# Expert weights of a mixture-of-experts layer in 168 transfers of 2 MB, one for each pair of units, in place of 336 transfers of 1 MB

## The chip, the cores and the metric

The kernel runs on one core of a Trainium2 chip. The time is the device time of one execution in microseconds (us), as the median of several runs. The five engines are TensorE (PE, with its weight load PEld), VectorE (DVE), ScalarE (ACT), GpSimd (POOL) and SyncE (SP). SP computes nothing here: it issues transfers from device memory (HBM) to the on-chip memory (SBUF), and its queue is written SPq.

## The reference

The kernel computes two layers of a decoder trunk on 256 tokens of width 1024, in float32. Each layer has a mixer (a gated delta rule on 4 heads and a stick-breaking attention on 8 heads) and then a channel mixer. In layer 0 that is a dense SwiGLU of width 2816. In layer 1 it is a SwiGLU of 8 experts of width 3584, each token going to the best 2:

```
def moe_swiglu(h, router_w, w_gate, w_up, w_down):
    logits = (xt @ router_w).astype(jnp.float32)
    top_val, top_idx = lax.top_k(logits, TOP_K)
    gates = jax.nn.softmax(top_val, axis=-1)
    combine = jnp.einsum("nk,nke->ne", gates, jax.nn.one_hot(top_idx, N_EXPERTS, dtype=jnp.float32))
    y = jnp.zeros((B * T, D), dtype=jnp.float32)
    for e in range(N_EXPERTS):
        y = y + combine[:, e:e + 1] * swiglu(xt, w_gate[e], w_up[e], w_down[e]).astype(jnp.float32)
```

The three weights of the experts are 8 x 3 x 1024 x 3584 numbers of 4 bytes, 352 MB in all, and each is read once.

## The kernel before

Everything is written out by hand: each engine has its own program, and semaphores join them. The expert stage starts after the output projection of layer 1. It works on one expert after another, and cuts its 3584 hidden columns into four chunks of 8, 8, 8 and 4 tiles of 128 (`MOE_TILES`). TensorE gathers up to 88 tokens of an expert, multiplies them by the gate and up weights of a chunk (`m_in`, L1119), later by its down weights (`m_down`, L1143), and at times transposes the result (L1157), adds it back to the tokens (`scatter_piece`, L1175, eight pieces in the first part of each expert but the first one's) and gathers the next expert's tokens (L1049).

The weights come in units of 1 MB: 128 partitions by 2048 numbers, 32 calls of TensorE each. `unit_queue` fixes the order of the 336 units, which is the order of their transfers and of their use. Sixteen buffers (`N_UNIT`) hold them in turn: twelve lie in the tensor `ring`, which the mixers and the dense layer used before in four slots of three units, and four in the tensor `late`, which the mixer of layer 1 leaves free later. The first 16 units are issued as these places come free (`first_free`), and unit n after that when TensorE has finished unit n - 16 (`unit_used`).

There is a second condition for unit n. The program of TensorE is longer than the engine holds, and its instructions are themselves brought in while it runs, in blocks; the kernel counts blocks of `PAGE` = 256 instructions. `page_turns` marks one call of TensorE shortly behind the start of each block, and this call raises the semaphore `page_turn`. `UNIT_TURN` says for each unit behind which such turn the transfer into its buffer may be issued, and lets at most two units go behind one turn:

```
if has_signal and signal_every == UNIT_CALLS:
    earliest = unit_turn[-TURN_UNITS] + 1 if len(unit_turn) >= TURN_UNITS else 1
    unit_turn.append(max(len(turns) + 1, earliest))
```

Worked out, this gives 172 turns. Behind each of them two units may go, but behind the turns 1, 14, 36, 50, 58, 79, 101, 114, 123 and 144 one. So behind turns 2 to 13 an odd unit and the next even one go together, behind turns 15 to 35 an even unit and the next odd one, and so on in turn.

Of the kernel before, what the change touches and what calls it, by code (L numbers as in the profile page):

```python
# [30 lines left out]
P = 128  # L31
D = 1024
# [16 lines left out]
SLOT = 2 * KD * FC + (FC // P) * D  # L49
NSLOT = 4  # L50
# [4 lines left out]
MOE_TILES = (8, 8, 8, 4)  # L55
# [16 lines left out]
FIRST_MOE = 2 * N_MIX + FFN_CH  # L72

UNIT = 2048
N_OWN = NSLOT * SLOT // UNIT
N_UNIT = N_OWN + 4
# [21 lines left out]
ROUND_UNITS = len(UNITS)  # L98
# [57 lines left out]
PAGE_TURNS, UNIT_TURN = page_turns()  # L156
# [52 lines left out]
def build(nc, x_in, consts, norm_mix_pre, norm_mix_post, norm_ffn_pre, norm_ffn_post, w_in, conv_w,  # L209
          dn_a_log, dn_dt_bias, dn_norm_w, sb_norm_w, w_out, ffn_gate, ffn_up, ffn_down, router_w,  # L210
          moe_gate, moe_up, moe_down, out):
    with ExitStack() as ctx:
        def sb(name, cols, dt=F32):
            return ctx.enter_context(nc.sbuf_tensor(name, [P, cols], dt))

        def sem(name):
            return ctx.enter_context(nc.semaphore(name))
# [7 lines left out]
        ring = sb("ring", NSLOT * SLOT)  # L225
# [7 lines left out]
        late = sb("late", (N_UNIT - N_OWN) * UNIT + 512)  # L233
# [73 lines left out]
        at = [0]  # L307
# [44 lines left out]

        ring_landed = [sem(f"ring_landed{i}") for i in range(NSLOT)]
        ring_used = sem("ring_used")
        unit_landed = [sem(f"unit_landed{i}") for i in range(N_UNIT)]
        unit_used = sem("unit_used")
        x_landed = [sem(f"x_landed{t}") for t in range(TT)]
        consts_landed, rows_landed, heads_landed, router_landed = (
# [45 lines left out]
        page_turn = sem("page_turn")  # L404
# [24 lines left out]
        def gate_up_down(n):  # L429
# [3 lines left out]
            d = s[:, 2 * KD * FC:SLOT].rearrange("p (i d) -> p i d", i=FC // P)  # L433
            return g, u, d

        def unit_of(n):

            i = n % N_UNIT
            if i < 3:
                return ring[:, 3 * SLOT + i * UNIT:3 * SLOT + (i + 1) * UNIT]  # L440
            if i < 6:
                return ring[:, (i - 3) * UNIT:(i - 2) * UNIT]
            if i < 10:
                return late[:, (i - 6) * UNIT:(i - 5) * UNIT]
            return ring[:, SLOT + (i - 10) * UNIT:SLOT + (i - 9) * UNIT]

        def gate_ks(c, j):

            nk = 2 * 8 // MOE_TILES[c]
            return range(j * nk, (j + 1) * nk)  # L450

        def gate_unit(n, c):
            return unit_of(n).rearrange("p (k f) -> p k f", f=MOE_TILES[c] * P)

        def down_unit(n):
            return unit_of(n).rearrange("p (i d) -> p i d", d=D)
# [9 lines left out]
        def per_round(r, n, a_round):  # L466
            return r * a_round + n
# [47 lines left out]
        def _(sp_):  # L515
# [44 lines left out]
            for c in range(FFN_CH):  # L560
                free_slot(FIRST_FFN + c)
                f = slice(c * FC, (c + 1) * FC)
# [2 lines left out]

            def first_free(n):

                if n < 6:
                    sp_.wait_ge(ring_used, FIRST_MOE - NSLOT + 1 + n // 3)
                elif n == 6:  # L570
                    sp_.wait_ge(dno_ps, DEPTH)
                    sp_.wait_ge(sb_ss, DEPTH * TT)
                elif n >= 10:
                    sp_.wait_ge(ring_used, FIRST_MOE - 1 + (n - 10) // 3)

            def moe_loads(r, first):
                for (kind, e, c, j), n in UNITS.items():
                    if first and n < N_UNIT:
                        first_free(n)
                    elif first:  # L580
                        sp_.wait_ge(unit_used, n - N_UNIT + 1)
                        sp_.wait_ge(page_turn, UNIT_TURN[n - N_UNIT])
                    else:
                        sp_.wait_ge(unit_used, per_round(r, n - N_UNIT + 1, ROUND_UNITS))
                    if kind == "d":
                        lo = (MOE_AT[c] + 2 * j) * P
                        dst = down_unit(n)
                        src = moe_down[0, e][lo:lo + 2 * P, :].rearrange("(i p) d -> p i d", p=P)
                    else:
                        f = slice(MOE_AT[c] * P, (MOE_AT[c] + MOE_TILES[c]) * P)  # L590
                        ks = gate_ks(c, j)
                        dst = gate_unit(n, c)
                        src = (moe_gate if kind == "g" else moe_up)[0, e][ks.start * P:ks.stop * P, f]\
                            .rearrange("(k p) f -> p k f", p=P)
                    sp_.dma_start(dst, src).then_inc(unit_landed[n % N_UNIT], 16)

            moe_loads(0, True)
            sp_.wait_ge(rounds_ready, 1)
            rounds = sp_.value_load(rounds_i[0:1, 0:1], min_val=1, max_val=3)
            with sp_.If(rounds > 1):  # L600
                with sp_.Fori(1, rounds) as r:
                    moe_loads(r, False)
# [9 lines left out]
        def _(pe):  # L612
# [479 lines left out]
                ins.then_inc(ohT_ps, 1)  # L1092

            def landed(r, n):
                pe.wait_ge(unit_landed[n % N_UNIT], per_round(r, 16 * (n // N_UNIT + 1), 16 * ROUND_UNITS // N_UNIT))

            def units_of(c, part):

# [1025 lines left out]
```

## Time and profile before

| | |
|---|---|
| median of 3 runs | 1599.26 us (1595.29 to 1600.52) |
| the profiled execution | 1602.32 us, its span 1600.5 us |
| granted TensorE clock, mean | 0.993 of full speed |
| PE busy | 1538.1 us, 96% of the span |
| expert stage, first to last call of L1119 and L1143 | about 642 us to 1582 us |

The span is the time from the first to the last instruction in the profile; the execution is 1.8 us longer than it. A busy PE is not PE at its peak, since matmuls overlap in it. An idle time "<-issue" is one in which the engine waited for nothing that the profile shows. The DMA share is the mean busy share of the 16 DMA engines; it can pass 1 by a little, since packets overlap.

### The profile page before, as it was taken

To read this page: it belongs to the slowest core of one execution; us is meant where nothing else is said; L and a number is where in the kernel's file an instruction comes from. 1 tells how busy PE (TensorE), PEld (TensorE's weight loads), DVE (VectorE), ACT (ScalarE), POOL (GpSimd) and SP (SyncE) were. 2 spreads that over 40 slices of the span, in tenths; PEclk is the share of its full clock that TensorE was granted. 3 is DMA by queue.
4 is the path that set the end of the run, shared out by engine and by line. 5 is a ranking of instruction groups with operands and counts; after the bars stand their busy time and mean duration, and the time that the engine had idled before them with its cause. 6 is when DMAs were issued, how large, how long until landed. Compare 5 with 4: busy or idle time off the path is not lost.

```text
span 1600.5 us, 54283 instructions
## 1 busy us (share of the span) xinstructions
PE 1538.1 (96%) x25845; PEld 1329.8 (83%) x25845; DVE 258.0 (16%) x489; ACT 179.0 (11%) x383; POOL 143.4 (9%) x167
## 2 busy tenths in 40 slices
PE   8999999999999999999999999999999999999998
PEld 7787587777687865989899999999999998998996
DVE  3433310000143435000010010010000000000002
ACT  3223120000231332100000000000000000000001
POOL 2243200000022532200000000000000000000000
PEclk9999999999999999999999999999999999999998
DMA  9213344444332145999999999999999999999970
GB/s 337 86 52 132 105 158 158 158 158 145 112 138 106 56 158 221 355 387 365 379 389 374 358 369 373 384 363 391 379 370 386 366 361 377 393 354 381 388 283 28
DMA packets 147947, 433.46 MB, mean 271 GB/s; under 512 B 9082, under 2 KB 33916, under 8 KB 147724
## 3 DMA queue, kind: packets, MB, share of 16 engines
q1 hardware_dynamic: 146720, 427.70, 71.6%
q8 instruction: 203, 3.33, 0.8%
q0 software_dynamic: 672, 2.14, 0.5%
q10 hardware_dynamic: 332, 0.13, 0.0%
q14 instruction: 20, 0.16, 0.0%
HBM read 428.89 MB, written 1.05 MB: 269 GB/s over the span
## 4 chain that ended last, share of the span: by engine, by line
PE 92%; issue 3%; DVE 2%; ACT 1%; POOL 1%; DMA 0%; ACTq 0%; DVEq 0%
PE ps L1119 35%; PE ps L1143 18%; PE ps L969 9%; PE ps L675 8%; PE ps L980 4%; PE ps L838 4%; PE ps L686 3%; PE ps L1175 2%; PE ps L1049 1%; PE ps L795 1%; PE ps L671 1%; PE ps L805 1%; PE ps L701 1%; PE ps L708 1%; PE ps L815 1%
## 5 line engine op out<-in xcount | busy, mean ns | idle before, releaser
L1143 PE MATMUL ps<-LT_sb,ring 128*64 128x88 f32 x5376 | 217.5, 240 | 11.4 <-issue 9.8
L1143 PEld LDWEIGHTS ps<-LT_sb,ring 128*64 128x64 f32 x5376 | 208.4, 137 | 21.1 <-issue 19.7
L1119 PE MATMUL ps<-wpost,ring 128*64 128x88 f32 x5376 | 215.4, 240 | 10.8 <-issue 9.2
L1119 PEld LDWEIGHTS ps<-wpost,ring 128*64 128x64 f32 x5376 | 207.8, 137 | 18.7 <-issue 16.8
L1119 PE MATMUL ps<-AT_sb,ring 128*64 128x88 f32 x5376 | 215.4, 240 | 7.7 <-issue 7.4
L1119 PEld LDWEIGHTS ps<-AT_sb,ring 128*64 128x64 f32 x5376 | 207.9, 137 | 16.2 <-issue 15.8
L969 PEld LDWEIGHTS ps<-hT_sb,ring 128*128 128x128 f32 x768 | 136.0, 190 | 24.7 <-issue 9.1
L969 PE MATMUL ps<-hT_sb,ring 128*128 128x256 f32 (+1 forms) x768 | 155.7, 362 | 0.0
L675 PE MATMUL ps<-hT_sb,ring 128*128 128x256 f32 x592 | 131.7, 380 | 0.0
L675 PEld LDWEIGHTS ps<-hT_sb,ring 128*128 128x128 f32 x592 | 111.1, 190 | 15.4 <-DVE late L1620 0.5
L1964 POOL TENSOR_SCALAR small<-small 128x1 f32<-128x1 f32 x16 | 3.9, 241 | 1204.9 <-ACT late L1498 935.5
L1479 ACT ACTIVATE BM<-ps 128x704 f32<-128x704 f32 (+1 forms) x32 | 21.9, 684 | 675.6 <-PE ps L1119 675.6
L1907 DVE TENSOR_TENSOR LT_sb<-BM,ps 128x704 f32<-128x704 f32 (+1 forms) x32 | 25.4, 793 | 417.0 <-PE ps L1119 417.0
L1119 PE MATMUL ps<-AT_sb,late 128*64 128x88 f32 x1792 | 72.1, 240 | 2.6 <-issue 2.6
L1143 PE MATMUL ps<-LT_sb,late 128*64 128x88 f32 x1792 | 72.5, 240 | 1.6 <-issue 1.2
L1119 PEld LDWEIGHTS ps<-AT_sb,late 128*64 128x64 f32 x1792 | 69.5, 137 | 5.4 <-issue 5.3
L1119 PE MATMUL ps<-wpost,late 128*64 128x88 f32 x1792 | 71.8, 240 | 2.0 <-issue 1.9
L1143 PEld LDWEIGHTS ps<-LT_sb,late 128*64 128x64 f32 x1792 | 69.6, 137 | 4.5 <-issue 4.3
L1119 PEld LDWEIGHTS ps<-wpost,late 128*64 128x64 f32 x1792 | 69.4, 137 | 4.3 <-issue 4.0
L1895 DVE SCALAR_TENSOR_TENSOR h_sb<-ps,small,h_sb 128x512 f32<-128x512 f32 x32 | 24.0, 751 | 294.8 <-PE ps L1175 290.3
L980 PE MATMUL ps<-ring,LT_sb 128*128 128x512 f32 x144 | 64.7, 592 | 0.0
L838 PE MATMUL ps<-ring,hT_sb 128*128 128x512 f32 x128 | 58.4, 607 | 1.7 <-ACT hT_sb L1432 1.7
(284 smaller groups left out, 1164.3 us busy)
## 6 DMA issues: line engine op xcount, KB each, us to landing
ring<-in_moe_w_gate SPq DMA_DIRECT2D x84, 1024.0 KB, 8.0
ring<-in_moe_w_up SPq DMA_DIRECT2D x84, 1024.0 KB, 8.0
ring<-in_moe_w_down SPq DMA_DIRECT2D x84, 1024.0 KB, 8.1
late<-in_moe_w_up SPq DMA_DIRECT2D x28, 1024.0 KB, 8.0
late<-in_moe_w_gate SPq DMA_DIRECT2D x28, 1024.0 KB, 8.9
late<-in_moe_w_down SPq DMA_DIRECT2D x28, 1024.0 KB, 7.8
ring<-in_ffn_w_gate SPq DMA_DIRECT2D x11, 1024.0 KB, 5.4
ring<-in_ffn_w_up SPq DMA_DIRECT2D x11, 1024.0 KB, 8.0
```

The source lines that it names most:

```text
L671: ins = mm(o[:, t * P:(t + 1) * P], w[:, k, col:col + P], hT[:, k, t * P:(t + 1) * P], start=(k == 0), stop=(k == KD - 1))
L675: ins = mm(o[:, 0:T], w[:, k, col:col + P], hT[:, k, :], start=(k == 0), stop=(k == KD - 1))
L686: ins = mm(o, hT[:, k, i * P:(i + 1) * P], w[:, k, col:col + 512], start=(k == 0), stop=(k == KD - 1))
L838: ins = mm(bank(4 + 2 * t + hf), mixT[:, k, t * P:(t + 1) * P], w[:, k, :], start=(k == 4), stop=(k == 3))
L969: ins = mm(bank(mt % 4)[:, which * T + lo:which * T + hi], w[:, k, i * P:(i + 1) * P], hT[:, k, lo:hi], start=(k == 0), stop=(k == KD - 1))
L980: ins = mm(bank(4 + 2 * t + half), ffn_hid[:, mt % 4, t * P:(t + 1) * P], d[:, i, half * 512:(half + 1) * 512], start=(mt == 0), stop=(mt ...
L1119: ins = mm(o[lo:lo + P // 2, :], w[:, i, m * P + lo:m * P + lo + P // 2], xgT[e % 2][:, k, :], start=(k == 0 and m % 4 == 0), stop=(k == K ...
L1143: ins = mm(o[lo:lo + P // 2, :], d[:, i, m * P + lo:m * P + lo + P // 2], moe_hid[:, 2 * j + i, :], start=(first and m % 4 == 0), stop=las ...
L1175: ins = mm(bank(6 + hf)[:, quarter * 256:(quarter + 1) * 256], onehotT[e % 2][:, t * P:(t + 1) * P], y_tok[:, (2 * hf + quarter) * 256:(2 ...
L1479: A(by_bank(moe_sg, c), tiles_of(0, c), ACT.Silu).then_inc(msg_ready, 1)
L1895: V.scalar_tensor_tensor(moe_yv[:, t, half(hf)], bank((6 if e < N_EXP - 1 else 2 * t) + hf), gate[:, t * N_EXP + e:t * N_EXP + e + 1], moe ...
L1907: V.tensor_tensor(by_bank(moe_hid, c), by_bank(moe_sg, c), tiles_of(2, c), ALU.mult).then_inc(mhid_ready, 1)
```

## The change

Two neighbouring units, n even and n + 1, become a pair. `pair_of` places the two side by side, and the order of the buffers moves for this: the first pair lies at the end of `ring`, the second at its start, the third and fourth in `late`, the others in the rest of `ring`. One transfer of 2 MB fills a pair, with the semaphore `pair_landed`; its rows in HBM are those of the two transfers before. It waits for the condition that the second unit of the pair had. TensorE waits once for a pair. The calls of TensorE and what they read of the weights stay the same, and so does the number of instructions in its program, 13638 as written, since the wait of the second unit rode on a matmul.

```diff
@@ -352,7 +352,7 @@
 
         ring_landed = [sem(f"ring_landed{i}") for i in range(NSLOT)]
         ring_used = sem("ring_used")
-        unit_landed = [sem(f"unit_landed{i}") for i in range(N_UNIT)]
+        pair_landed = [sem(f"pair_landed{i}") for i in range(N_UNIT // 2)]
         unit_used = sem("unit_used")
         x_landed = [sem(f"x_landed{t}") for t in range(TT)]
         consts_landed, rows_landed, heads_landed, router_landed = (
@@ -433,16 +433,16 @@
             d = s[:, 2 * KD * FC:SLOT].rearrange("p (i d) -> p i d", i=FC // P)
             return g, u, d
 
+        def pair_of(n):
+
+            i = n // 2 % (N_UNIT // 2)
+            if i in (2, 3):
+                return late[:, (i - 2) * 2 * UNIT:(i - 1) * 2 * UNIT]
+            at = (N_OWN - 2, 0)[i] if i < 2 else 2 * (i - 3)
+            return ring[:, at * UNIT:(at + 2) * UNIT]
+
         def unit_of(n):
-
-            i = n % N_UNIT
-            if i < 3:
-                return ring[:, 3 * SLOT + i * UNIT:3 * SLOT + (i + 1) * UNIT]
-            if i < 6:
-                return ring[:, (i - 3) * UNIT:(i - 2) * UNIT]
-            if i < 10:
-                return late[:, (i - 6) * UNIT:(i - 5) * UNIT]
-            return ring[:, SLOT + (i - 10) * UNIT:SLOT + (i - 9) * UNIT]
+            return pair_of(n)[:, n % 2 * UNIT:(n % 2 + 1) * UNIT]
 
         def gate_ks(c, j):
 
@@ -565,34 +565,35 @@
 
             def first_free(n):
 
-                if n < 6:
-                    sp_.wait_ge(ring_used, FIRST_MOE - NSLOT + 1 + n // 3)
-                elif n == 6:
+                if n < 4:
+                    sp_.wait_ge(ring_used, FIRST_MOE - NSLOT + 1 + n // 2)
+                elif n == 4:
                     sp_.wait_ge(dno_ps, DEPTH)
                     sp_.wait_ge(sb_ss, DEPTH * TT)
-                elif n >= 10:
-                    sp_.wait_ge(ring_used, FIRST_MOE - 1 + (n - 10) // 3)
+                elif n >= 8:
+                    sp_.wait_ge(ring_used, FIRST_MOE - 1 + (n - 8) // 4)
 
             def moe_loads(r, first):
                 for (kind, e, c, j), n in UNITS.items():
+                    if n % 2:
+                        continue
                     if first and n < N_UNIT:
                         first_free(n)
                     elif first:
-                        sp_.wait_ge(unit_used, n - N_UNIT + 1)
-                        sp_.wait_ge(page_turn, UNIT_TURN[n - N_UNIT])
+                        sp_.wait_ge(unit_used, n + 1 - N_UNIT + 1)
+                        sp_.wait_ge(page_turn, UNIT_TURN[n + 1 - N_UNIT])
                     else:
-                        sp_.wait_ge(unit_used, per_round(r, n - N_UNIT + 1, ROUND_UNITS))
+                        sp_.wait_ge(unit_used, per_round(r, n + 1 - N_UNIT + 1, ROUND_UNITS))
                     if kind == "d":
                         lo = (MOE_AT[c] + 2 * j) * P
-                        dst = down_unit(n)
-                        src = moe_down[0, e][lo:lo + 2 * P, :].rearrange("(i p) d -> p i d", p=P)
+                        dst = pair_of(n).rearrange("p (i d) -> p i d", d=D)
+                        src = moe_down[0, e][lo:lo + 4 * P, :].rearrange("(i p) d -> p i d", p=P)
                     else:
                         f = slice(MOE_AT[c] * P, (MOE_AT[c] + MOE_TILES[c]) * P)
-                        ks = gate_ks(c, j)
-                        dst = gate_unit(n, c)
-                        src = (moe_gate if kind == "g" else moe_up)[0, e][ks.start * P:ks.stop * P, f]\
-                            .rearrange("(k p) f -> p k f", p=P)
-                    sp_.dma_start(dst, src).then_inc(unit_landed[n % N_UNIT], 16)
+                        lo, hi = gate_ks(c, j).start * P, gate_ks(c, j + 1).stop * P
+                        dst = pair_of(n).rearrange("p (k f) -> p k f", f=MOE_TILES[c] * P)
+                        src = (moe_gate if kind == "g" else moe_up)[0, e][lo:hi, f].rearrange("(k p) f -> p k f", p=P)
+                    sp_.dma_start(dst, src).then_inc(pair_landed[n // 2 % (N_UNIT // 2)], 16)
 
             moe_loads(0, True)
             sp_.wait_ge(rounds_ready, 1)
@@ -1092,7 +1093,9 @@
                 ins.then_inc(ohT_ps, 1)
 
             def landed(r, n):
-                pe.wait_ge(unit_landed[n % N_UNIT], per_round(r, 16 * (n // N_UNIT + 1), 16 * ROUND_UNITS // N_UNIT))
+                if n % 2 == 0:
+                    pe.wait_ge(pair_landed[n // 2 % (N_UNIT // 2)],
+                               per_round(r, 16 * (n // N_UNIT + 1), 16 * ROUND_UNITS // N_UNIT))
 
             def units_of(c, part):
 
```

How the order of SP's transfers moves at the start of the expert stage, where the first 16 units go into free places (rows of SP, equal ones that follow each other merged; the shape is partitions x rows x numbers). Before:

```order
L595 DMA ring<-in_moe_w_gate 128x2x1024 [waits ring_used] x4
L595 DMA ring<-in_moe_w_up 128x2x1024 [waits ring_used] x2
L595 DMA late<-in_moe_w_up 128x2x1024 [waits sb_ss,dno_ps]
L595 DMA late<-in_moe_w_up 128x2x1024
L595 DMA late<-in_moe_w_gate 128x2x1024 x2
L595 DMA ring<-in_moe_w_gate 128x2x1024 [waits ring_used] x2
L595 DMA ring<-in_moe_w_down 128x2x1024 [waits ring_used] x4
L595 DMA ring<-in_moe_w_up 128x2x1024 [waits page_turn,unit_used] x4
```

And after the change:

```order
L596 DMA ring<-in_moe_w_gate 128x4x1024 [waits ring_used] x2
L596 DMA late<-in_moe_w_up 128x4x1024 [waits sb_ss,dno_ps]
L596 DMA late<-in_moe_w_up 128x4x1024
L596 DMA ring<-in_moe_w_gate 128x4x1024 [waits ring_used] x2
L596 DMA ring<-in_moe_w_down 128x4x1024 [waits ring_used] x2
L596 DMA ring<-in_moe_w_up 128x4x1024 [waits page_turn,unit_used] x2
```

Six units went ahead of the four in `late`, now four do; six units waited for the end of the output projection, now eight do.

On TensorE, at the start of the first expert (its program's order, with the semaphore that a call waits for), before:

```order
L1119 MATMUL ps<-wpost,ring 64x88 [waits unit_landed4]
L1119 MATMUL ps<-wpost,ring 64x88 x31
L1119 MATMUL ps<-wpost,ring 64x88 [waits unit_landed5]
L1119 MATMUL ps<-wpost,ring 64x88 x31
L1119 MATMUL ps<-wpost,late 64x88 [waits unit_landed6]
L1119 MATMUL ps<-wpost,late 64x88 x31
L1119 MATMUL ps<-wpost,late 64x88 [waits unit_landed7]
L1119 MATMUL ps<-wpost,late 64x88 x31
```

And after the change:

```order
L1122 MATMUL ps<-wpost,late 64x88 [waits pair_landed2]
L1122 MATMUL ps<-wpost,late 64x88 x63
L1122 MATMUL ps<-wpost,late 64x88 [waits pair_landed3]
L1122 MATMUL ps<-wpost,late 64x88 x63
L1122 MATMUL ps<-wpost,ring 64x88 [waits pair_landed4,msg_ready]
L1122 MATMUL ps<-wpost,ring 64x88 x63
```

Every second wait is gone, and the same 32 calls a unit stand between the others.

## Rows read from the trace of the kernel before

**Rows 1.** The page: parts 1 to 3, and a line of part 6.

```profile
PE 1538.1 (96%) x25845; PEld 1329.8 (83%) x25845; DVE 258.0 (16%) x489; ACT 179.0 (11%) x383; POOL 143.4 (9%) x167
...
DMA  9213344444332145999999999999999999999970
...
q1 hardware_dynamic: 146720, 427.70, 71.6%
q8 instruction: 203, 3.33, 0.8%
...
ring<-in_moe_w_gate SPq DMA_DIRECT2D x84, 1024.0 KB, 8.0
```

**Rows 2.** Windows: start:end length, busy us of PE, PEld, DVE, ACT, POOL, PEclk, DMA share, GB/s.

```profile
633.00:645.00 12.00, 10.25 (x181) 7.84 (x181) 7.56 (x36) 3.62 (x8) 3.05 (x4) 1.00 1.02 412
700.30:1500.00 799.70, 769.17 (x18661) 732.10 (x18659) 56.76 (x91) 28.48 (x48) 0.00 (x0) 1.00 0.99 375
721.60:741.50 19.90, 18.73 (x490) 18.43 (x487) 0.89 (x1) 0.46 (x1) 0.00 (x0) 1.00 0.94 345
646.50:1576.30 929.80, 895.51 (x21796) 853.66 (x21792) 64.10 (x104) 36.70 (x58) 6.67 (x4) 1.00 0.96 364
```

**Rows 3.** Waits in 646.5 to 1576.3 us: SP's queue, then PE.

```profile
SPq L582 <- PE ps L1119: 495.6, 108, 13.4
SPq L582 <- PE ps L1143: 242.0, 53, 5.3
...
PE ps L1119 <- issue: 21.0, 32, 1.4
PE ps L1143 <- issue: 11.0, 16, 1.2
```

**Rows 4.** Timeline of PE: start, length, what, count (64 records are one unit).

```profile
737.15 6.08 PE L1143 MATMUL ps<-LT_sb,ring 128*64 128x88 f32 x148 [1.17 <-issue]
...
803.35 5.07 PE L1119 MATMUL ps<-AT_sb,ring 128*64 128x88 f32 x128
808.35 0.70 PE L1175 MATMUL ps<-BM,X_sb 88*128 88x256 f32 x2
808.98 5.07 PE L1119 MATMUL ps<-AT_sb,ring 128*64 128x88 f32 x128
```

**Rows 5.** Timeline of SP's queue; DMA queues in 731.0 to 734.8 us, then 734.8 to 736.0.

```profile
731.37 7.13 SPq L595 DMA_DIRECT2D ring<-in_moe_w_up  x4
...
q1 hardware_dynamic: 387, 1.49, 102.2%
...
q1 hardware_dynamic: 119, 0.45, 95.0%
q8 instruction: 1, 0.02, 5.3%
```

**Rows 6.** Timeline of SP's queue, 706 to 722.5 us.

```profile
710.74 6.01 SPq L595 DMA_DIRECT2D late<-in_moe_w_gate  x2
721.62 1.74 SPq L595 DMA_DIRECT2D ring<-in_moe_w_gate  x2
```

**Rows 7.** Timeline of SP's queue, then of PE, at the stage's start.

```profile
598.71 0.88 SPq L595 DMA_DIRECT2D late<-in_moe_w_up  x2
...
629.54 0.88 SPq L595 DMA_DIRECT2D ring<-in_moe_w_gate  x2
630.46 2.61 SPq L595 DMA_DIRECT2D ring<-in_moe_w_down  x4
...
642.47 9.93 PE L1119 MATMUL ps<-wpost,ring 128*64 128x88 f32 x256 [1.17 <-DVE wpost L1879]
```

**Rows 8.** DMA queues in 639.5 to 642.4 us, then in 642.4 to 643.8.

```profile
q1 hardware_dynamic: 309, 1.19, 102.6%
...
q1 hardware_dynamic: 135, 0.55, 98.5%
q8 instruction: 1, 0.02, 4.8%
```

## The prediction

> **What bounds the kernel now.** I read the page first. TensorE is busy for 96% of the span, and in the expert stage, the last 25 or so of the 40 slices, the DMA engines are at nine tenths or more too [rows 1]. So both are near their limit, and the windows have to tell which. Over the middle of the stage the DMA share is 0.99 at 375 GB/s, with PE busy for 769.17 of 799.7 us [rows 2]. A pair of units is 2.097 MB, 5.59 us at 375 GB/s. TensorE alone needs 9.93 us for the first four units [rows 7], 4.96 us for two, and 5.63 us for two and a scatter piece, from 803.35 to 808.98 [rows 4]. There are 56 such pieces (seven experts, eight each). So of the 172 instruction blocks, of about two units each, 56 have a piece, and there TensorE is the slower; in the other 116, which I call plain, the transfers are the slower by up to 0.63 us a block.
>
> One would expect TensorE to wait there for weights. It does not. SP waits for TensorE, 737.6 us in all at L582 [rows 3], a unit lands 8.0 us after its issue [rows 1], and its use comes only some seven blocks of 929.8/171 = 5.44 us later [rows 2]. TensorE's idle time is all "<-issue", 32.0 us in 48 waits [rows 3]; the window row gives 929.8 - 895.5 = 34.3 us for PE and 76.1 us for the weight load, part of which is idle at changes of work. The cause is in the DMA rows. A transfer of q8 is 3.33 MB / 203 = 16.4 KB and takes 0.008 x 1600.5 x 16 / 203 = 1.0 us on one engine [rows 1]: that is a block of 256 instructions. SP issues at 731.37, just behind a turn; no q8 packet is served up to 734.8, while q1, the weights, fills all engines; the block comes between 734.8 and 736.0 [rows 5], and TensorE, which has run out of instructions, goes on at 737.15 after 1.17 us of idle time [rows 4]. So the weights hold TensorE back through its instructions. The queue left over at a turn is about 8.0 - 5.59 = 2.4 us of transfers [rows 1, 2], the block comes behind that, and when the queue grows past some 3 us, TensorE stalls, issues later, and the queue shrinks. In plain blocks the time is thus the DMA engines' time, and everything that adds to the queue at a turn comes back as a stall.
>
> The Trainium skill speaks of this in "Runtime: NRT & Kernel Launch", section "Instruction fetch mechanics": instructions come in blocks of 16 KiB, 256 of them, and crossing into a new block costs little and is mostly hidden. The size agrees with the 16.4 KB above; "mostly hidden" does not, with at least 34 us of idle time. By that rule this change would come out at 0, by the rows at the sum below.
>
> **The change part by part.**
>
> *Waits and instructions.* TensorE's program keeps its 13638 instructions, so the turns stay at the same calls. 168 waits for weights go; none of them ended an idle time [rows 3], so they are worth 0. SP has half the issues; it waits for TensorE most of the time [rows 3], so 0.
>
> *Later issue.* The first unit of a pair may now go one turn later than before, some 5.5 us. Its cover is the lead of about seven blocks, 38 us, less the landing of 8 us: 30 us, so 0. Without that cover each pair would cost up to 5 us.
>
> *The stage's start.* Six units went at 629.54 to 633.07 (two and four) [rows 7]; now eight do. At 412 GB/s [rows 2] a unit takes 2.55 us, so the queue is full some 5 us longer, to about 652 us, over the start of TensorE's loop at 642.47 [rows 7]. A block of instructions that was wanted near there was not served from 639.5 to 642.4, while 1.19 MB of weights went, and was served in 642.4 to 643.8 [rows 8], before the six units were through. I read that it gets in between two transfers on its engine. If it waits for the rest of one and the whole of the next, it waits up to 2.55 us more for the next with 1 MB and up to 5.1 us with 2 MB. Bounds: 0 (the delay falls in the 1.17 us that TensorE waits for VectorE and in the block in hand) and 6 us (two blocks late). I take +3, since two blocks fall into the longer queue and one is likely covered.
>
> *Turns with one unit.* Behind turns 14, 50, 79, 114 and 144 two units now go, not one; behind 1, 36, 58, 101 and 123 none. The first kind adds a unit of 2.55 to 2.80 us to the queue. Turn 14 is the issue near 716.4, alone in front of the two at 721.62 [rows 6]. What it gave back was partly spent: with the short queue the next 19.9 us ran at 345 GB/s [rows 2], 19.9 x 30/375 = 1.6 us of transfers lost. So the loss is 2.8 - 1.6 = 1.2 us, at most 2.8. It counts at 14, 79 and 144, which plain blocks follow, 3.6 to 8.4 us; 50 and 114 lie among scatter pieces, where TensorE is the slower: 0. At the four later turns without a unit the queue of 2.4 us runs dry within 5.44 us. One unit there kept it just alive, so what is relieved is small and what is lost is a slow start: between -0.3 us and +1.6 us each, taken as +0.35. Sum +5, bounds +2 and +14.
>
> *The rate.* Against 5.09 us at 412 GB/s a pair loses 0.50 us [rows 2], of which the block fetch is 1.0/16 = 0.06 and 0.44 something else. If that is paid for each transfer, half of it goes: 0.22 x 116 plain blocks = -26 us. If it is paid for each start on a short queue, one a turn before and after, it is 0. Inside 633 to 645 us four or so transfers follow each other at full rate, so a boundary alone costs nothing; I stay near 0 and take -3.
>
> Sum: 3 + 5 - 3 = +5 us. On the profiled execution that is 1602.3 (span 1600.5 and 1.8 around it) to 1607.3. It stood 3.1 us above the median, so I add the +5 to the median: about 1604.5 us.
>
> **The rivals.**
>
> *Small terms cancel.* The start costs nothing, or a little is saved at the boundaries: +1, so 1600 us. For it: each term is a few us among 930.
>
> *Each transfer has its price* (the other side). The lost 0.44 us belongs to transfers. At two thirds of the -26 us in place of my -3, it is 1599.3 + 8 - 17 = 1590 us. For it: nothing isolates a single transfer in a short queue. Against it: the full rate in 633 to 645. It decides the sign from 8/116 = 0.07 us saved a plain block.
>
> *Blocks wait for longer transfers.* The block in hand then waits for the whole of a 2 MB transfer, 5.09 us, and 5.09 + 1.0 is over the 4.96 us of a plain block. TensorE would stall until the queue at a turn is near nothing, and a short queue runs at 345 GB/s, 6.08 us a pair [rows 2]: up to 0.49 x 116 = 57 us, and at half of it 1628 us. For it: the wait in [rows 8]. Against it: at a turn only the rest of one pair is queued, however it is cut.
>
> The Trainium skill bears on this one, in "DMA: Bandwidth & Descriptors", section "Queues, rings and completion order": a DMA engine changes between queues only when it has drained a whole packet, typically 9 to 17 descriptors and at most 64. The waits for the blocks fit that [rows 5, 8]. By it one engine's share of a 2 MB transfer, 512 rows of 4 KB over 16 engines, may be one packet of 32, and this rival is what would follow.
>
> **Chances.** A measurement of this kernel tells about 0.3%, 4.8 us, from no change. The forecast, +2 to +12 us, has 0.42, of which 0.32 lies above +4.8. The cancelling has 0.28, all within. The price by transfer has 0.18, the longer waits 0.12. So slower 0.44, same 0.38, faster 0.18. The range of 8 in 10 goes from 1588 (the whole -26 us is left out, its two thirds kept) to 1616 us (the bound +14 and 3 more, the longer waits left out in their larger part); that of the forecast alone is 1601 to 1612.
>
> **What the profile after would show.** In windows of plain blocks the rate stays near 375 GB/s; at 385 or more the price by transfer is right, under 365 the longer waits. PE's idle "<-issue" rises by about 5 us from 32; by tens, with the longer waits. The window from 721.6 on has a rate over 345 GB/s, and a lower one stands behind turn 36. The first loop call at about 642.5 is unchanged, but a stall appears in its first two blocks. A wait of TensorE for a transfer would make the prediction wrong, as it would overthrow the lead of 30 us.

## The result

| | ratio to before | 95% interval | median, us |
|---|---|---|---|
| before | 1 | | 1599.02 (1591.73 to 1603.25, 20 runs) |
| after | 1.0039 | 1.0023 to 1.0054 | 1605.57 (1599.65 to 1617.3, 20 runs) |

The changed kernel is slower by 0.39%, 6.2 us by the ratio. The forecast was +5 us, 1604.5 us; the change lies in its range. The runs of one kernel spread by more than this difference, so every number of 3 us below leans on many runs, and one profiled execution cannot carry it alone. The granted clock explains little of it: in the repetition on one chip (after_again) its mean is 0.9955 against 0.9963 in the runs of before, and among the runs of one kernel 0.001 of it goes with some 1.2 us, so by this estimate it is worth about 1 us of the 6.

The page of after, the lines that answer to those of before [rows 1] (engine: busy us, share of the span, instructions; the busy tenths of the DMA engines in 40 slices; queue: packets, MB, share; a load with its KB and median us to landing):

```profile
span 1601.6 us, 53955 instructions
...
PE 1535.5 (96%) x25845; PEld 1328.5 (83%) x25845; DVE 258.1 (16%) x489; ACT 179.0 (11%) x383; POOL 143.3 (9%) x167
...
DMA  9213344444332225999998999999999999999980
...
q1 hardware_dynamic: 144032, 427.69, 71.5%
q8 instruction: 203, 3.33, 0.8%
...
ring<-in_moe_w_gate SPq DMA_DIRECT2D x42, 2048.0 KB, 10.0
```

The profiled execution took 1603.41 us with a span of 1601.6 us, some 2 us below the median of its kernel, while that of before lay 3 us above its own. The two spans differ by only 1.1 us for this reason. A load of 2 MB lands 10.0 us after its issue, where 1 MB took 8.0 [rows 1].

The windows that answer to [rows 2] (columns as there):

```profile
633.00:645.00 12.00, 10.30 (x150) 7.10 (x151) 7.20 (x36) 3.25 (x8) 1.98 (x4) 0.86 1.03 413
700.30:1500.00 799.70, 766.51 (x18610) 730.26 (x18612) 56.78 (x91) 28.43 (x48) 0.00 (x0) 1.00 0.99 376
721.60:741.50 19.90, 17.55 (x447) 16.96 (x444) 0.89 (x1) 0.46 (x1) 0.00 (x0) 1.00 1.01 394
646.50:1576.30 929.80, 891.92 (x21724) 850.86 (x21722) 64.11 (x104) 37.38 (x59) 7.75 (x4) 1.00 0.97 366
```

The rate in the middle of the stage is 376 GB/s and was 375. So the price of 0.22 us for a transfer is not given back, and nothing like 57 us is lost to longer waits. By the signs that the prediction announced, neither of these two rivals is there in its full size. What changes is *when* the rate is high: 394 GB/s behind turn 14, where it was 345.

The waits of SP's queue and of PE in 646.5 to 1576.3 us, which answer to [rows 3]:

```profile
SPq L584 <- PE ps L1122: 576.2, 107, 19.2
SPq L584 <- PE ps L1146: 249.3, 49, 6.1
...
PE ps L1122 <- issue: 24.5, 36, 1.7
PE ps L1146 <- issue: 12.8, 22, 1.4
```

TensorE's idle time "<-issue" is 37.3 us in 58 waits and was 32.0 in 48 [rows 3]. That is the announced rise of 5 us, but it proves little: half_mb below, which takes the time of before, has 37.3 us in 56 waits. Still no wait of TensorE ends with a transfer of weights.

The stage's start, which answers to [rows 7] (timeline of SP's queue, then of PE):

```profile
629.17 0.92 SPq L596 DMA_DIRECT2D ring<-in_moe_w_gate  x2
630.14 3.20 SPq L596 DMA_DIRECT2D ring<-in_moe_w_down  x2
652.57 5.47 SPq L596 DMA_DIRECT2D ring<-in_moe_w_up  x2
...
643.55 10.01 PE L1122 MATMUL ps<-wpost,ring 128*64 128x88 f32 x256 [1.17 <-DVE wpost L1882]
653.72 9.93 PE L1122 MATMUL ps<-wpost,late 128*64 128x88 f32 x256
```

The eight units go at 629.17 to 633.34, and TensorE's first 512 calls take 10.01 and 9.93 us without a stall. It starts 1.1 us later than before, but that came from ahead of the stage: the window of 633 to 645 has a granted clock of 0.86 in this execution, and had 1.00 in that of before.

How long the first block of instructions had to wait there can be read from the DMA queues (in 629.1 to 641.0 us, in 641.0 to 643.5, in 643.5 to 644.6):

```profile
q1 hardware_dynamic: 1031, 4.15, 91.2%
...
q1 hardware_dynamic: 263, 1.02, 101.7%
...
q1 hardware_dynamic: 105, 0.43, 98.1%
q8 instruction: 1, 0.02, 6.1%
```

Counted along its records, TensorE passes into a new block at 641.00 (its instruction 194 of each 256, where its stalls stand in all these kernels; "entry" below). Of the 8.39 MB in the four transfers, 4.15 are through by then and 4.2 are still queued. Yet the next block of instructions comes after 2.50 us and 1.02 MB more, not after the 10 us that 4.2 MB take. In before, the entry at 639.93 had 2.8 MB of 1 MB transfers queued, and the block came after 2.58 us, in the window from 642.4 on of [rows 8].

The turns themselves show best in windows of 19.9 us. Of before, behind the turns 14, 50, 79, 114 and 144, which had one unit, and then behind 36, 58, 101 and 123:

```profile
716.30:736.20 19.90, 19.67 (x506) 19.19 (x502) 0.89 (x1) 0.84 (x2) 0.00 (x0) 1.00 0.93 339
912.60:932.50 19.90, 19.90 (x458) 18.15 (x454) 1.10 (x3) 0.00 (x0) 0.00 (x0) 1.00 0.92 318
1072.10:1092.00 19.90, 19.80 (x511) 19.42 (x509) 0.89 (x1) 0.84 (x2) 0.00 (x0) 1.00 0.96 353
1262.00:1281.90 19.90, 19.90 (x458) 18.22 (x452) 1.85 (x4) 0.76 (x1) 0.00 (x0) 1.00 0.91 342
1426.50:1446.40 19.90, 19.56 (x506) 19.25 (x501) 0.89 (x1) 0.84 (x2) 0.00 (x0) 1.00 0.90 332
836.50:856.40 19.90, 19.67 (x505) 19.18 (x500) 0.89 (x1) 0.84 (x2) 0.00 (x0) 1.00 0.94 354
956.70:976.60 19.90, 19.76 (x508) 19.37 (x507) 0.89 (x1) 0.84 (x2) 0.00 (x0) 1.00 0.98 368
1191.80:1211.70 19.90, 19.69 (x506) 19.27 (x500) 0.89 (x1) 0.84 (x2) 0.00 (x0) 1.00 0.99 368
1310.80:1330.70 19.90, 19.31 (x496) 18.89 (x493) 0.89 (x1) 0.84 (x2) 0.00 (x0) 1.00 0.91 343
```

The same nine of after, where the first five turns have a pair and the last four nothing:

```profile
716.80:736.70 19.90, 19.00 (x482) 18.37 (x478) 0.89 (x1) 0.53 (x2) 0.00 (x0) 1.00 1.02 397
916.00:935.90 19.90, 19.54 (x456) 17.99 (x452) 1.10 (x3) 0.00 (x0) 0.00 (x0) 1.00 0.99 370
1074.40:1094.30 19.90, 19.16 (x493) 18.78 (x489) 0.89 (x1) 0.69 (x2) 0.00 (x0) 1.00 1.03 385
1263.80:1283.70 19.90, 19.90 (x458) 18.15 (x454) 1.85 (x4) 0.76 (x1) 0.00 (x0) 1.00 1.01 384
1427.30:1447.20 19.90, 18.92 (x485) 18.39 (x482) 0.89 (x1) 0.38 (x1) 0.00 (x0) 1.00 1.00 383
839.10:859.00 19.90, 19.34 (x496) 18.92 (x493) 0.89 (x1) 0.84 (x2) 0.00 (x0) 1.00 0.78 292
960.40:980.30 19.90, 19.90 (x514) 19.64 (x513) 0.89 (x1) 0.84 (x2) 0.00 (x0) 1.00 0.83 305
1194.00:1213.90 19.90, 19.81 (x504) 19.22 (x500) 0.89 (x1) 0.84 (x2) 0.00 (x0) 1.00 0.84 319
1312.70:1332.60 19.90, 19.26 (x499) 18.95 (x497) 0.89 (x1) 0.84 (x2) 0.00 (x0) 1.00 0.79 294
```

The last column is the point. Behind the first five it goes from 318 to 353, mean 337, to 370 to 397, mean 384. Over 19.9 us that is 0.93 MB more, about one unit (1.05 MB). Behind the last four it falls from a mean of 358 to 303 GB/s, 1.1 MB less, with a DMA share of 0.78 to 0.84: there the queue of weights runs dry. In the three of the first five that plain blocks follow (first, third and fifth row), PE was busy for 19.67, 19.80 and 19.56 us and now is for 19.00, 19.16 and 18.92, so it is idle for 0.65 us more in each.

### The profile page after: what moved, and what is told of

Its sections match the earlier page's. It is cut to its first block, busy times and chain, and to the rows that moved or that the text cites. A ratio compares the mean times of both kernels' runs of the same rounds, so it can differ in the third digit from the quotient of the medians.

```text
span 1601.6 us, 53955 instructions
## 1 busy us (share of the span) xinstructions
PE 1535.5 (96%) x25845; PEld 1328.5 (83%) x25845; DVE 258.1 (16%) x489; ACT 179.0 (11%) x383; POOL 143.3 (9%) x167
## 3 DMA queue, kind: packets, MB, share of 16 engines
HBM read 428.89 MB, written 1.05 MB: 268 GB/s over the span
## 4 chain that ended last, share of the span: by engine, by line
PE 92%; issue 3%; DVE 2%; ACT 1%; POOL 1%; DMA 0%; ACTq 0%; DVEq 0%
PE ps L1122 35%; PE ps L1146 18%; PE ps L970 9%; PE ps L676 8%; PE ps L981 4%; PE ps L839 4%; PE ps L687 3%; PE ps L1178 2%; PE ps L1050 1%; PE ps L796 1%; PE ps L806 1%; PE ps L702 1%; PE ps L709 1%; PE ps L672 1%; PE ps L816 1%
```

## The experiments

Each was timed beside before on the same chip. The ratios are to before; 0.001 is 1.6 us.

| | ratio | 95% interval | median, us (runs) |
|---|---|---|---|
| after_again | 1.0042 | 1.0023 to 1.0061 | 1605.57 (12) |
| pair_timing_1mb | 1.0019 | 0.9999 to 1.0039 | 1601.08 (12) |
| start_as_before | 1.0041 | 1.0021 to 1.0061 | 1606.66 (12) |
| half_mb | 1.0001 | 0.9981 to 1.0021 | 1598.18 (12) |
| pair_timing_again | 1.0020 | 1.0001 to 1.0040 | 1601.58 (12) |
| size_only | 1.0151 | 1.0120 to 1.0181 | 1625.15 (6) |
| no_turn_1mb | 1.0223 | 1.0192 to 1.0254 | 1636.21 (4) |
| no_turn_2mb | 1.0431 | 1.0402 to 1.0461 | 1669.60 (4) |
| size_alone | 1.0024 | 1.0005 to 1.0043 | 1604.82 (12) |
| drift_1mb | 1.0189 | 1.0158 to 1.0220 | 1628.89 (4) |
| mark_2_2mb | 1.0042 | 1.0027 to 1.0056 | 1608.06 (12) |
| mark_20_2mb | 1.0076 | 1.0053 to 1.0098 | 1613.30 (6) |

**The changed kernel again (after_again).**

> The changed kernel once more, to compare the others with on the same chip. Measured so far: 1.0039 of the kernel before, 1.0023 to 1.0054. Both theories expect 1.002 to 1.006 here.

1.0042: the loss is there a second time, with a mean of 1605.9 us.

**The start (start_as_before).** The first 16 units go as 1 MB each at the points that they had before, ten of them early; all later ones as in after:

```diff
+            def first_units():
+                by_n = {n: u for u, n in UNITS.items()}
+                for n in (0, 1, 15, 2, 3, 8, 4, 5, 6, 7, 9, 10, 11, 12, 13, 14):
...
+                    sp_.dma_start(dst, src).then_inc(pair_landed[n // 2], 16)
             def moe_loads(r, first):
+                if first:
+                    first_units()
```

> The changed kernel, but its first 16 units go in transfers of 1 MB and at the points of the kernel before: ten ahead of the end of the output projection and six behind it, not eight and eight. Theory as predicted (the start costs 3 us): 3 us under the changed kernel, some 1.002 of the kernel before. Rival (the start is covered, as the trace after suggests, where no stall stands in the first blocks): the same as the changed kernel within 1 us, 1.004.

1.0041 beside 1.0042 for after_again, with means of 1606.0 and 1605.9 us that are uncertain by some 2 us against each other. The start costs nothing that these runs can show, and the +3 us of the prediction are hardly there.

**The timing of after with the size of before (pair_timing_1mb, and again as pair_timing_again).** Both halves of a pair are issued one after the other under the pair's condition, as two transfers of 1 MB:

```diff
                     if n % 2:
-                        continue
-                    if first and n < N_UNIT:
+                        pass
+                    elif first and n < N_UNIT:
...
-                        dst = pair_of(n).rearrange("p (i d) -> p i d", d=D)
-                        src = moe_down[0, e][lo:lo + 4 * P, :].rearrange("(i p) d -> p i d", p=P)
+                        dst = unit_of(n).rearrange("p (i d) -> p i d", d=D)
+                        src = moe_down[0, e][lo:lo + 2 * P, :].rearrange("(i p) d -> p i d", p=P)
```

> 336 transfers of 1 MB, into the buffers of the change and under its conditions: both units of a pair wait for the condition of the second. Only the size of a transfer is put back. Theory (when the pairs are issued costs, in the turns with one unit and at the start): the same as the changed kernel, 1.003 to 1.005, +5 to +8 us over the kernel before. Rival (the size of a transfer costs): the same as the kernel before, 0.999 to 1.001. If a larger transfer is cheaper by itself, this one is slower than the changed kernel.

> The changed kernel with its 168 transfers cut in 336 of 1 MB, both halves of a pair issued under the pair's condition: the timing of the changed kernel, the size of before. A second measurement, since the first (ratio 1.0019, interval 0.9999 to 1.0039) lies between the two theories. Theory that the timing alone costs it (two units behind turns 14, 50, 79, 114, 144, none behind four others): ratio 1.0039, about 1605.5 us. Theory that the size of the transfers alone costs it: 1.0000, about 1599. Half and half: 1.0019, about 1602.

1.0019 and 1.0020, 24 runs in all with a mean of 1601.9 us, between before (1599.3 and 1599.1 us, the means of its runs beside them) and after (1605.8 and 1605.9 us, 32 runs in all). The runs of one kernel scatter by about 4 us here, so the difference to after, 4.0 us, is uncertain by some 2 us, and that to before, about 3 us (2.7 by these means, 3.1 by the ratios), by nearly as much. So each of two parts of the change has a share: the size of the transfers about 3 to 4 us, and the rest about 3 us. The rest is the timing, together with the new order of the buffers and TensorE's one wait for a pair, which this kernel has too. PE's idle time "<-issue" and the middle of the stage in the profiled execution of pair_timing_again:

```profile
PE ps L1122 <- issue: 19.1, 30, 1.7
PE ps L1146 <- issue: 15.6, 20, 1.5
...
700.30:1500.00 799.70, 768.66 (x18691) 733.11 (x18687) 56.80 (x91) 28.43 (x48) 0.00 (x0) 1.00 0.99 377
```

The idle time is 34.7 us in 50 waits, between the 32.0 of before [rows 3] and the 37.3 of after, but with the 37.3 of half_mb it ranks nothing. The rate is 377 GB/s, and 379 in pair_timing_1mb; the three kernels with 2 MB and the same turns (after, after_again, start_as_before) have 376, 375 and 373. One execution each: the rate points the same way as the times, no more, since before itself has 375.

**Still smaller transfers (half_mb).** Before, with each unit in two transfers of 0.5 MB:

```diff
-                    sp_.dma_start(dst, src).then_inc(unit_landed[n % N_UNIT], 16)
+                    rows = dst.shape[1] // 2
+                    for i in range(2):
+                        part = slice(i * rows, (i + 1) * rows)
+                        sp_.dma_start(dst[:, part, :], src[:, part, :]).then_inc(unit_landed[n % N_UNIT], 16)
```

> The kernel before with each unit in two transfers of 0.5 MB, issued under the same condition one behind the other: 672 transfers. Theory (a block of instructions waits for the rest of the transfer in service on its engine and for one whole one behind it, so smaller transfers let it in earlier): a block waits at most some 2.6 us, idle time by issue falls from 32 us to under 15, the queue may grow, and the rate rises from 375 GB/s; 0.975 to 0.995, so 1560 to 1591 us. Rival (a block waits for everything that is queued when it is asked for, whatever the cut): the same as the kernel before, 0.998 to 1.003, with the idle time unchanged.

1.0001: from 1 to 0.5 MB nothing changes, in either direction. The idle time "<-issue" is 37.3 us in 56 waits, where the second branch had expected the 32.0 of before, so this sum moves by 5 us without a change of the time.

The traces show why the cut does not matter. Over the whole stage (646.5 to 1576.3 us) a block of instructions comes on average 2.56 us after the entry before it, in before 2.52 and in after 2.61. In 84 of 171 blocks of half_mb more than 1.05 MB of weights, two of its transfers, went in between; in before it is 84 of 172 blocks, in after 84 of 171. With 0.9 to 1.2 MB queued at the entry the mean, up to 1500 us, is 2.63 us in half_mb, 2.53 in before and 2.43 in after, and with 1.2 to 1.5 MB it is 3.09, 3.10 and 3.19. So the wait goes with the bytes that are queued, whether they are cut in 0.5, 1 or 2 MB. The start of the stage shows that this has an end: with 2.1 MB queued (half_mb), 2.8 (before) or 4.2 (after) the block comes after 2.50 to 2.58 us.

**The size at the timing of before (size_only).** Where two neighbours went behind the same turn before, one transfer takes both:

```diff
+        two = (n >= N_UNIT and n + 1 < ROUND_UNITS and UNIT_TURN[n - N_UNIT] == UNIT_TURN[n + 1 - N_UNIT]
+               and kinds[n] == kinds[n + 1] and unit_at(n + 1) == unit_at(n) + 1)
```

> The timing of before, and the size of after where it can be had: every unit is issued behind the turn that it has before, and where two neighbours go behind the same turn, belong to the same weight and lie side by side, one transfer of 2 MB takes both (97 of 336 units' worth of pairs, so 58% of the 168 pairs; the other 142 units stay alone at 1 MB). The buffers lie as after the change. If the timing alone costs the 6 us: ratio 1.0000, about 1599 us. If the size alone costs them: 58% of 6.3 us, so 1.0023, about 1602.7 us. If each of the two costs half: 1.0012, about 1601 us.

1.0151, three times as much as any theory had. The cause was not in the transfers. The values that TensorE waits for are computed in registers, and with uneven counts for each semaphore 90 more of these instructions stood in its program (165 records of that kind in the trace, against 75). The table that places the calls which raise `page_turn` knows nothing of them. Counted along the records of TensorE, its stalls come at instruction 193 or 194 of each 256 in all these kernels. The turn is raised at 217 on average in before and after, but drifts from 219 to 28 of the following 256 in size_only. So the run tells nothing of the size, and something else of the turns, which drift_1mb tests.

**The size once more (size_alone).** The counts are evened out, 96 pairs go as 2 MB, and the marks are moved by 0.75 instructions for each expert, 6 in all, since the program was taken to be 6 shorter:

```diff
+_, UNIT_TURN = page_turns()
+WAITS["g1"] -= 0.75
+PAGE_TURNS, _ = page_turns()
...
+                pe.wait_ge(unit_landed[NTH[n] % N_UNIT],
+                           per_round(r, 16 * (NTH[n] // N_UNIT + 1), 16 * N_TRANSFER // N_UNIT))
```

> The timing of before, and 96 of its 168 pairs in one transfer of 2 MB where both units go behind the same turn, as in size_only. That one gave 1.0151, which neither theory had; its TensorE program turned out some 100 register instructions longer, so that the calls that raise page_turn drifted against the blocks of instructions, from place 218 in a block to place 29 of the next one. Here the counts of the semaphores are evened out, so the program has 6 instructions fewer than before, and the marks follow the blocks. If the size of the transfers costs nothing and the timing costs the 6 us: ratio 1.0000, about 1599 us. If the size alone costs them: 57% of 6.3 us, 1.0023, about 1602.7 us; half and half 1.0012. If the drift was not the cause of size_only's loss: 1.0151, about 1624 us, again.

1.0024, which is what the size alone was to give. But the program came out one instruction longer, since 7 more instructions for semaphores (290 against 283 records) had come in, so that the marks drifted again, from 218 to 227 in the block, some 5 later than in before on average. By mark_20_2mb below, 12 later cost 5.4 us, so up to 2.3 of the 3.8 us may be this. The run speaks for a share of the size, and its amount is open between 1.5 and 3.8 us for 57% of the pairs.

**Where in its block the turn is raised (drift_1mb, mark_2_2mb, mark_20_2mb).** The first is before with a table that counts 12 instructions fewer for each expert, the others are after with all marks 6 earlier and 12 later; which unit goes behind which turn is held as it was:

```diff
-PAGE_TURNS, UNIT_TURN = page_turns()
+_, UNIT_TURN = page_turns()
+WAITS["g1"] -= 12
+PAGE_TURNS, _ = page_turns()
```

```diff
+_, UNIT_TURN = page_turns()
+TURN_MARKS = (2,)
+PAGE_TURNS, _ = page_turns()
```

> The kernel before, with 1 MB transfers and its own timing of units to turns; only the calls that raise page_turn move: the table that places them counts 12 instructions fewer per expert, so the turn comes later and later in its block of instructions, by some 12 per expert and 96 in the end, as in size_only. If the place of the turn in the block was what cost size_only its 24 us: ratio about 1.015, 1623 us, with a rate in the middle of the stage near 367 in place of 375 GB/s. If the mixture of 1 MB and 2 MB transfers was: 1.000, 1599 us.

> The changed kernel with every turn marked 6 instructions earlier in its block (0.12 us), which unit goes behind which turn being the same. If the changed kernel is slower because its transfers reach the queue before the block of instructions is asked for, earlier marks make it worse: 1.006 to 1.010, 1609 to 1615 us. If it is slower because the queue runs shorter between the turns, earlier marks give some of it back: 1.001 to 1.003, 1601 to 1604 us. If the place of the mark does not matter: 1.004, as the changed kernel.

> The changed kernel with every turn marked 12 instructions later in its block (0.23 us). If transfers that are queued before the block of instructions is asked for are what costs it: 1.000 to 1.003, 1599 to 1604 us. If the shorter queue is what costs: each of 116 plain blocks loses up to 0.23 us of transfers, 1.006 to 1.02, 1609 to 1630 us. If neither: 1.004.

drift_1mb: 1.0189, with all transfers of 1 MB. So the place of the turn explains most of size_only: its turns are some 35 instructions late on average, and at the price of drift_1mb that is about 21 of its 24 us, an estimate. The middle of the stage in drift_1mb:

```profile
700.30:1500.00 799.70, 750.05 (x18083) 711.31 (x18081) 54.64 (x88) 27.41 (x46) 0.00 (x0) 1.00 0.97 363
```

and in mark_20_2mb:

```profile
700.30:1500.00 799.70, 757.50 (x18357) 720.41 (x18353) 55.18 (x89) 27.84 (x47) 0.00 (x0) 1.00 0.98 370
```

363 and 370 GB/s, in place of 375 and 376. In drift_1mb the turn comes at 218 at first and at about 58 of the next 256 in the end, some 48 instructions late on average, 0.93 us at 4.96 us for 256. The loss of 30 us is 0.18 us for each of 172 turns. In mark_20_2mb 12 instructions or 0.23 us cost 5.4 us more than after_again, 0.03 us a turn. The 5.4 us are uncertain by some 3. 6 instructions earlier change nothing (1.0042 in both), within 2 us. So weights that come later behind the turn cost time, with a lower DMA rate, and of the two readings offered, the shorter queue is the one that fits mark_20_2mb. Whether after is slower because its transfers are late stays open. By the 5.4 us for 12 instructions, mark_2_2mb had some 3 us to gain at most, hardly more than can be told, and in ten of its turns the mark fell at instruction 193, so that the pair went ahead of the block.

**No turns at all (no_turn_1mb, no_turn_2mb).** The wait for `page_turn` is left out of before and of after, so a transfer is issued as soon as TensorE has used up its place:

```diff
                         sp_.wait_ge(unit_used, n - N_UNIT + 1)
-                        sp_.wait_ge(page_turn, UNIT_TURN[n - N_UNIT])
```

> The kernel before without the wait for page_turn: a unit is issued as soon as its buffer is used up, so the queue of weights stays as deep as the 16 buffers allow and every block of instructions meets a queue of many units. If a block only waits for the transfer in work on its engine and the next one (what the prediction read), it waits up to 5 us with 1 MB, little more than before, and the time is 1600 to 1615 us, or less, since the deeper queue runs at 412 instead of 375 GB/s. If it waits for everything that is queued when it is asked for, it waits for as much as the queue holds, TensorE stalls at every block and the time is above 1650 us.

> The changed kernel without the wait for page_turn: a deep queue of 2 MB transfers. If a block of instructions waits for the transfer in work and the next one, it waits up to 10 us here and twice as long as in the same kernel with 1 MB, and the time is above that one's by up to 5 us a block, several hundred us. If it waits for everything queued when it is asked for, the size does not matter and the two kernels are within 1% of each other.

1.0223 and 1.0431, 36 and 69 us. The middle of the stage, with 1 MB:

```profile
700.30:1500.00 799.70, 744.97 (x17933) 706.18 (x17931) 54.67 (x88) 26.67 (x45) 0.00 (x0) 1.00 0.98 360
```

and with 2 MB:

```profile
700.30:1500.00 799.70, 726.39 (x17288) 683.30 (x17284) 53.37 (x87) 26.19 (x44) 0.00 (x0) 1.00 0.94 347
```

My expectation was wrong in its picture: the queue of transfers does not grow to 16 buffers, since a transfer is issued only once its place is used up, and the DMA rate is lower than before (360 and 347 GB/s), not higher. So the two branches as I wrote them were not told apart by the time. The rows of no_turn_2mb tell them apart (SP's timeline; PE's timeline; the DMA queues in 1103.9 to 1108.7 us; the same in 1108.7 to 1109.9):

```profile
1102.99 0.37 SPq L595 DMA_DIRECT2D ring<-in_moe_w_gate  x1
1109.10 0.37 SPq L595 DMA_DIRECT2D ring<-in_moe_w_down  x1
...
1105.21 5.07 PE L1121 MATMUL ps<-AT_sb,ring 128*64 128x88 f32 x128 [0.59 <-issue]
1111.15 5.07 PE L1121 MATMUL ps<-AT_sb,ring 128*64 128x88 f32 x127 [0.87 <-issue]
...
q1 hardware_dynamic: 418, 1.70, 98.9%
...
q1 hardware_dynamic: 109, 0.40, 82.4%
q8 instruction: 1, 0.02, 5.2%
```

One pair is issued at 1102.99. TensorE passes into a new block behind the stall that ends at 1105.21. From 1103.9 to 1108.7 the weights move 1.70 MB at a DMA share of 98.9% and no instruction block is served. It comes between 1108.7 and 1109.9, 3.6 us after the entry, when some 1.8 of the pair's 2.1 MB have gone. TensorE runs dry and goes on at 1111.15. So a block of instructions waits for most of the pair that is queued ahead of it. Only this one pair is queued, so these rows do not tell the whole queue from the transfer in work; half_mb above does. With issue at any time more bytes stand ahead of a block: at the entry over 1.5 MB are queued before 84 of 145 blocks up to 1500 us here and before 28 of 151 in no_turn_1mb, and the mean wait from the entry is 3.43 us against 2.92. TensorE's stall then delays the use of the next units and with it their issue. This fits the 69 us against 36, though the two kernels also differ in the pair's condition, so not all of the difference need be the size. The Trainium skill, "DMA: Bandwidth & Descriptors", section "Queues, rings and completion order", says that an engine changes between queues when it has drained a packet, typically 9 to 17 descriptors and at most 64. By the row 418 pieces of about 4 KB went meanwhile, 26 on each of 16 engines; that is more than the typical number and less than the largest, so these rows bear out a long wait and do not tell the rule from plain order of arrival. If a block is asked for at the entry before it, plain order of arrival does not hold at the start of the stage in after, where the block was served with some 3.2 MB of earlier transfers still to go. What the limit is, no run here isolates. half_mb, with the same bytes in more transfers, gained nothing.

## Why the prediction was right, and where it was not

**What bounds the kernel: right.** In after as in before TensorE never waits for weights, its idle time is "<-issue", and the DMA rate in the middle is the same to 1 GB/s. That the weights hold TensorE back through its instructions is shown by no_turn_2mb in single rows, and by 36 and 69 us when the turns are left out.

**Waits, instructions and later issue at 0: right.** TensorE has the same 25845 calls, and no idle time ends at a transfer.

**The stage's start, +3: wrong, it is 0 within some 2 us.** start_as_before takes it out and stays at 1.0041. Of the two ends that I had given, 0 to 6 us, the lower one holds. The step that failed is "one is likely covered, the other not", and the wait behind it, "up to 2.55 us more for the next with 1 MB and up to 5.1 us with 2 MB". The announced stall in the first two blocks did not come: the first 512 calls run without any, though the queue is full. The block waits 2.50 us from the entry with 4.2 MB of 2 MB transfers queued, and 2.58 us with 2.8 MB of 1 MB transfers.

**Turns with one unit, +5: the mechanism is seen, the size is about +3.** The nine windows show it turn by turn: 384 in place of 337 GB/s behind the five, 303 in place of 358 behind the four, with 0.65 us more of idle TensorE behind each of the three that I had counted at 1.2 us. These idle times are of one execution; half_mb, with the turns of before, is idle for 0.85 to 1.60 us behind the same three, so they illustrate and don't prove. The evidence is in the times: pair_timing_1mb and its repetition, with transfers of 1 MB, give 1.0019 and 1.0020, +3.1 us, inside the bounds of +2 and +14. That it is just these nine turns was not isolated: about half of the pairs also have their first unit a turn later, and the order of the buffers and the waits of TensorE are those of after.

**The rate, -3: wrong in sign.** I had set bounds of 0 and -26 us and nothing above 0. The size of the transfers costs 3 to 4 us (after against pair_timing, 4.0 us, uncertain by 2), where half the size brings nothing (half_mb 1.0001). So the saving for each transfer does not show, and the rival that each transfer has its price falls. What the 3 to 4 us are is not settled. A share of *Blocks wait for longer transfers* is not seen: for the same bytes queued a block waits about as long in after as in before, and more than 4 us in 3 blocks of each (in 4 and 7 of the two pair_timing kernels). It is not excluded either, since 3.5 us are 0.02 us for each of 172 blocks, less than these means can tell. That such long waits are rare fits a block that is asked for about when the one before it is entered, some 24 instructions ahead of the turn, so that the pair of that turn is queued behind it.

**The reading of [rows 8]** that a block waits for the rest of one transfer and the whole of the next is wrong: then half_mb would have shortened the waits. In the middle of the stage the wait grows with the bytes queued at the entry, up to some 1.5 MB, however they are cut, and the start shows that the whole of a longer queue need not go first. The entry stands for the moment at which the block is asked for; no row shows that moment itself, but in the three profiled starts above the block follows the entry by 2.50 to 2.58 us, while its distance from the first of the queued transfers is 13.0 to 14.3 us.

**The sum.** 0 + 3 + 3.5 = 6.5 us is what the runs make of 3 + 5 - 3 = 5. That the total came out right is in good part luck: the start was 3 us too high, the turns about 2 too high and the rate about 6.5 too low, and these errors nearly cancel.

None of the twelve kernels is faster than before, so there is no better version to offer.

## What to carry to other kernels

When the instructions of an engine come through the same DMA engines as its data, ask for every transfer whether it is queued ahead of the next block of instructions or behind it: that mattered far more here than the number of transfers. From 0.5 to 1 MB a transfer the time did not change at all, and 2 MB was a little slower, so with the DMA engines at a share of 0.99 the merger saved nothing here, and it coarsened the one thing that was tuned, when how much is issued. And an edit that adds a few instructions to an engine's program can move such a schedule by more than the edit itself: count the instructions before reading the time.

## What was not expected of the hardware

- The place of the signal inside a block of 256 instructions: 0.23 us later at every turn cost 5.4 us (mark_20_2mb against after_again), a drift of 0.93 us on average 30 us (drift_1mb), while 0.12 us earlier made no difference that could be told.
- With a dry queue behind a turn without a pair the DMA share fell to 0.78 and the rate to 292 GB/s over 19.9 us, and TensorE lost almost nothing in it: PE was busy for 19.34 us, where it had been 19.67. Where such a lull is paid for, no row shows.
- A block of instructions of 16 KB waits for the bytes that are queued ahead of it, 3.6 us behind most of a pair in no_turn_2mb. But a queue of 2.1 to 4.2 MB at the stage's start held it up for only 2.5 us, and the cut in transfers of 0.5, 1 or 2 MB made no difference to the wait.
